# Second mixer: inputs with tokens on partitions, matrix-engine transposes in place of rearranging through memory, direct term in the kernel matrices

## The reference

```
u, z = split(rmsnorm(h) @ w_in, 2)              # 1024 columns each; u: 64 groups of 16 channels
x[t] = a * x[t-1] + B u[t]                      # complex, 64 states for each group
y = Re(C x) + d_skip * u                        # the last part is the direct term
y = gelu(y);  ga, gb = split(y @ w_glu, 2)
h = h + (ga * sigmoid(gb) * silu(z)) @ w_out
```

## Time and profile before

| what | value |
|---|---|
| median of three runs | 2049.64 us (2049.35 to 2049.81) |
| the profiled execution's own time | 2053.18 us |
| its span, first to last instruction | 2051.4 us |
| mean granted PE clock | 0.955 |
| PE busy | 1826.9 us (89%) |
| DVE, ACT, POOL busy | 1005.5, 816.8, 303.3 us |
| from the end of attention to the last output tile | 461.4 to 523.4 us |
| from there to the first glu product | 523.4 to 684.7 us |

### The profile page before, as it was taken

The page is one execution under the profiler, slowest core; times in us unless marked ns, Lnnn a source line. Parts: engine busy times, 40 slices in busy tenths (PEclk is TensorE's granted clock), DMA queues, the critical chain, the costliest instruction groups (busy, mean ns, idle before and its releaser), DMA issues.

```text
span 2051.4 us, 23580 instructions
## 1 busy us (share of the span) xinstructions
PE 1826.9 (89%) x9454; PEld 1450.1 (71%) x9454; DVE 1005.5 (49%) x1694; ACT 816.8 (40%) x1348; POOL 303.3 (15%) x376
## 2 busy tenths in 40 slices
PE   3488699997996999999799999999999969999996
PEld 2366578775775787786487777887777748888885
DVE  7647845665564446434434454445544364334323
ACT  4034356763313424333425545256632443223222
POOL 1347432546000000000000000012200021111000
PEclk9789799998998999999999999999999979999998
DMA  3154231005667422321032221321122212233231
GB/s 108 47 168 144 99 98 42 12 1 157 156 157 167 132 84 92 105 95 48 21 116 78 82 83 62 100 69 61 63 82 92 83 41 93 92 103 100 85 95 59
DMA packets 79230, 183.37 MB, mean 89 GB/s; under 512 B 24449, under 2 KB 35585, under 8 KB 77329
## 3 DMA queue, kind: packets, MB, share of 16 engines
q1 hardware_dynamic: 79120, 181.87, 28.7%
HBM read 165.58 MB, written 16.25 MB: 89 GB/s over the span
## 4 chain that ended last, share of the span: by engine, by line
PE 66%; DVE 17%; ACT 8%; DMA 4%; issue 2%; POOL 2%; SPq 1%; DVEq 0%; ACTq 0%; POOLq 0%
PE bank L822 16%; PE bank L823 16%; PE bank L824 15%; DVE wlo L1720 2%; PE bank L861 2%; PE bank L862 2%; PE bank L863 2%; PE bank L1003 2%; PE bank L981 2%; ACT whi L1249 1%; POOL Ps L2473 1%; ACT Ps L1619 1%; DVE Pb L1842 1%; DVE CA L1688 1%; PE bank L842 1%
## 5 line engine op out<-in xcount | busy, mean ns | idle before, releaser
L1720 DVE TENSOR_TENSOR wlo<-wraw,whi 128x1024 fp32r<-128x1024 f32 (+1 forms) x262 | 327.5, 1253 | 344.1 <-ACT whi L1249 342.7
L822 PE MATMUL bank<-Hh,whi 128*128 128x512 f32 (+2 forms) x1136 | 461.2, 406 | 24.0 <-DVE wlo L1720 13.2
L823 PE MATMUL bank<-Hl,whi 128*128 128x512 f32 (+2 forms) x1136 | 448.6, 395 | 0.0
L824 PE MATMUL bank<-Hh,wlo 128*128 128x512 f32 (+2 forms) x1136 | 448.2, 395 | 0.0
L1249 ACT ACTIVATE whi<-wraw 128x1024 fp32r<-128x1024 f32 (+1 forms) x262 | 271.1, 1040 | 373.0 <-PE bank L824 260.1
L822 PEld LDWEIGHTS bank<-Hh,whi 128*128 128x128 f32 (+2 forms) x1136 | 215.5, 190 | 84.5 <-DVE qs L1786 11.8
L824 PEld LDWEIGHTS bank<-Hh,wlo 128*128 128x128 f32 (+2 forms) x1136 | 215.3, 189 | 48.9 <-issue 0.6
L823 PEld LDWEIGHTS bank<-Hl,whi 128*128 128x128 f32 (+2 forms) x1136 | 215.8, 190 | 47.5 <-issue 2.7
L2466 POOL TENSOR_SCALAR bs<-dist 128x256 f32<-128x256 f32 x16 | 7.3, 457 | 831.8 <-DMA dist<-in_c_dist 831.1
L822 PE MATMUL bank<-Bh,whi 128*128 128x512 f32 x256 | 103.1, 403 | 2.2 <-DVE Bl L2244 2.2
L824 PE MATMUL bank<-Bh,wlo 128*128 128x512 f32 x256 | 102.1, 399 | 0.0
(11 more groups left out here) (368 smaller groups left out, 3044.7 us busy)
## 6 DMA issues: line engine op xcount, KB each, us to landing
wraw<-in_w_o SPq DMA_DIRECT2D x24, 512.0 KB, 3.5
wraw<-in_w_bgate SPq DMA_DIRECT2D x24, 512.0 KB, 3.4
wraw<-in_w_branch SPq DMA_DIRECT2D x24, 512.0 KB, 3.5
wraw<-in_w_fg SPq DMA_DIRECT2D x22, 512.0 KB, 3.4
wraw<-in_w_fu SPq DMA_DIRECT2D x22, 512.0 KB, 3.4
wraw<-in_w_s SPq DMA_DIRECT2D x16, 512.0 KB, 4.1
wraw<-in_w_glu SPq DMA_DIRECT2D x16, 512.0 KB, 3.6
wraw<-in_w_fd SPq DMA_DIRECT2D x16, 512.0 KB, 3.5
```

The source lines that it names most:

```text
L822: pe.matmul(o, wh[:, cols], hi(k), start=k == 0, stop=False)
L823: pe.matmul(o, wh[:, cols], lo(k), start=False, stop=False)
L824: m = pe.matmul(o, wl[:, cols], hi(k), start=False, stop=k == K - 1)
L1720: dve.tensor_tensor(c.wlo[q][:, 0:n], c.raw[i % RR][:, 0:n], c.whi[q][:, 0:n].bitcast(F32), S_).then_inc(*up(DID, ("wlo", i)))
```

## The change

The columns of `u` are computed the other way round: `tok_twin` takes 128 tokens as the stationary operand and 256 weight columns as the moving one, so that tokens lie on partitions. Four such steps `u0` to `u3` of 96 matmuls each take the place of eight `u` tiles. ACT evicts each bank with four copies (`ev_su`) into `Z`, with the factor 1/rms, which `rsS` has turned onto partitions; 16 transposes of 64x128 (`rows`) and two copies (ACT, DVE) give `U`. No memory is passed. The outputs are copied to `Yo` in a layout with 64 partitions, in four copies, and 16 transposes of 64x128 give y with channels on partitions; gelu reads it from PSUM. The direct term is added to the kernel matrix before it is stored (`prep_k` on DVE), so `finish` is gone. The shifted copies of `scratch_K` are made in memory during attention (`expand`), and `mT` comes in one DMA. `mW` has two buffers. `x_again` fetches one part of `X` per output tile, in that tile's step, and the first fetches come between these steps. Some working tiles move to other addresses.

```diff
+    def tok_twin(self, w, m, src):
+
+        keys = [(w, m, i) for i in range(2)]
+        for key in keys:
+            self.bank.take(key)
+        for j in range(2):
+            i = self.piece(w, (m, j), 0, 1024)
+            self.step("tok_twin", keys, i, j, src)
...
+            self.step("x_again", t)
             self.evict(("w_o0", t))
             self.step("split_h1", t)
             self.square("h1", t, 0, t == 0)
+            for kind, n, b in (("fetch_w", 2, 0), ("fetch_m", 3, 0), ("fetch_w", 5, 1)):
+                if t == n:
+                    self.step(kind, b)
...
+            if i in (16, 24, 32, 40):
+                self.step("expand", i // 8 - 2)
         self.drain()
-        self.step("x_again")
...
-        self.pair([("w_s5", 0), ("w_s5", 1)], "h1")
-        self.inv("h1", 0, 7, 0, 1.0 / D, "rs")
-
-        def u_tile(k):
-            if k > 1:
-                self.gemm("w_s5", k, "h1")
-            self.evict(("w_s5", k))
+
+        def inputs(b):
+            keys = self.tok_twin("w_su", b, "h1")
+            if b == 0:
+                self.inv("h1", 0, 7, 0, 1.0 / D, "rs")
+                self.early = keys
+                return
+            if b == 1:
+                self.bank.take("rsS")
+                self.step("rsS")
+                self.bank.give("rsS")
+                for key in self.early:
+                    self.evict(key)
+            for key in keys:
+                self.evict(key)
 
         def rows(b):
+            for i in range(2):
+                self.bank.take(("ut", b, i))
             self.step("rows", b)
+            for i in range(2):
+                self.bank.give(("ut", b, i))
...
-        order = ("u0 u1 r0 u2 u3 r1 s0 u4 w1 u5 r2 o0 s1 u6 w2 m2 u7 r3 t0 o1 s2 z0 w3 z1 m3 f0 t1 o2 s3 y0 z2 z3 f1 y1 "
-                 "t2 o3 z4 f2 y2 t3 z5 z6 z7 f3 y3")
+        fns = dict(u=inputs, r=rows, s=states, o=outputs, t=turned, z=z_tile, y=split_y, w=fetch_w, m=fetch_m)
+        order = ("u0 m1 u1 r0 s0 u2 r1 s1 w2 o0 u3 r2 s2 w3 m2 t0 o1 z0 r3 s3 m3 t1 o2 y0 z1 y1 z2 t2 y2 o3 z3 t3 y3 "
+                 "z4 z5 z6 z7")
...
+    def tok_twin(keys, i, j, src):
+        hi, lo = c.moving[src]
+        wh, wl = c.whi[plan.ring[i]], c.wlo[plan.ring[i]]
+        on.wait_ge(*at("wlo", i))
+        for t in range(4):
+            o = bank(keys[t // 2])[:, (t % 2) * 256:(t % 2) * 256 + 256]
+            if j == 0:
+                on.wait_ge(*before(plan.bank, keys[t // 2]))
+            rows = slice(t * 128, t * 128 + 128)
+            for kk in range(4):
+                k = j * 4 + kk
+                on.wait_ge(*at("lo", src, k))
...
+            done = [("used", i)] if t == 3 else []
+            if j == 1 and t % 2:
+                done.append(("tile", keys[t // 2]))
+            if done:
+                m.then_inc(*up(PE, *done))
...
+    def rsS():
+        b = bank("rsS")
+        on.wait_ge(*before(plan.bank, "rsS"))
+        on.wait_ge(*at("inv", "h1"))
+        for t in range(4):
+            for a in range(2):
+                x = pe.matmul(b[a * 64:a * 64 + 64, t:t + 1], c.rs[:, :].rearrange("p (n s) -> p s n", s=8)[:, 2 * t + a, :],
+                              c.ident[:, 0:1], start=True, stop=True)
+        x.then_inc(*up(PE, ("rsS",)))
+
+    def rows(b):
+        for i in range(2):
+            u = bank(("ut", b, i))
+            on.wait_ge(*before(plan.bank, ("ut", b, i)))
+            on.wait_ge(*at("Z", b, 1))
+            for g in range(8):
+                x = pe.transpose(u[:, g * 64:g * 64 + 64], c.Z[:, 8 * i + g, :, :].rearrange("p s n -> p (s n)"),
+                                 c.ident[0:64, 0:64])
+            x.then_inc(*up(PE, ("ut", b, i)))
...
-            for q in range(4):
-                x = pe.transpose(y[:, q * 128:q * 128 + 128], c.Yo[:, i, q * 128:q * 128 + 128], c.ident[:, :])
+            for k in range(8):
+                x = pe.transpose(y[:, k * 64:k * 64 + 64], c.Yo[:, i, k, :, :, :].rearrange("p q h n -> p (q h n)"),
+                                 c.ident[0:64, 0:64])
...
-        copy(c.Kp[:, :, 8:16, :].rearrange("p q k n -> p q (k n)"), k.rearrange("p (q n) -> p q n", q=4)).then_inc(
-            *up(DID, ("Kp", b), ("freed", ("kk", b))))
+        copy(c.Kp[:, :, 9:16, :].rearrange("p q k n -> p q (k n)"), k.rearrange("p (q n) -> p q n", q=4)[:, :, 16:128]).then_inc(
+            *up(DID, ("Kp", b)))
...
+    def ev_su(key):
+        _, b, i = key
+        on.wait_ge(*at("tile", key))
+        on.wait_ge(*at("rsSc"))
+        if b:
+            on.wait_ge(*at("ut", b - 1, 1))
+        for t in (2 * i, 2 * i + 1):
+            for a in range(2):
+                half = slice(a * 64, a * 64 + 64)
+                x = copy(c.Z[:, :, 2 * t + a, :],
+                         bank(key)[half, (t % 2) * 256:(t % 2) * 256 + 256].rearrange("p (g n) -> p g n", n=16),
+                         scale=c.rsS[half, t:t + 1])
+        x.then_inc(*up(DID, ("Z", b, i), ("freed", key)))
+
+    def rows(b):
+        on.wait_ge(*at("ut", b, 0))
+        copy(c.U[b][:, 0:8, :].rearrange("p g n -> p (g n)"), bank(("ut", b, 0))).then_inc(
+            *up(DID, ("U", b, 0), ("freed", ("ut", b, 0))))
...
-            copy(c.Yo[:, i, :], bank(("y", b, i))).then_inc(*up(DID, ("Yo", b, i), ("freed", ("y", b, i))))
+            for h in range(2):
+                half = slice(h * 64, h * 64 + 64)
+                x = copy(c.Yo[:, i, :, :, h, :].rearrange("p k q n -> p q k n"),
+                         bank(("y", b, i))[half, :].rearrange("p (q k n) -> p q k n", q=4, k=8))
+            x.then_inc(*up(DID, ("Yo", b, i), ("freed", ("y", b, i))))
 
     def turned(b):
         for i in range(2):
             on.wait_ge(*at("yt", b, i))
-            if b:
-                on.wait_ge(*at("dy", b - 1))
-            copy(c.Yt[:, 8 * i:8 * i + 8, :].rearrange("p g n -> p (g n)"), bank(("yt", b, i))).then_inc(
-                *up(DID, ("Yt", b, i), ("freed", ("yt", b, i))))
-
+            act.activation(c.Y[:, 2 * b + i, :], bank(("yt", b, i)), ACT.Gelu_apprx_tanh).then_inc(
+                *up(DID, ("gelu", 2 * b + i), ("freed", ("yt", b, i))))
...
+        dve.tensor_tensor(c.Kp[:, :, 8, :], k[:, :, 0:16], c.skip[:, b, :, :], A_).then_inc(
+            *up(DID, ("Kd", b), ("freed", ("kk", b))))
+
+    def rsS():
+        on.wait_ge(*at("rsS"))
+        dve.tensor_copy(c.rsS, bank("rsS")[:, 0:4]).then_inc(*up(DID, ("rsSc",), ("freed", "rsS")))
+
+    def rows(b):
+        on.wait_ge(*at("ut", b, 1))
+        dve.tensor_copy(c.U[b][:, 8:16, :].rearrange("p g n -> p (g n)"), bank(("ut", b, 1))).then_inc(
+            *up(DID, ("U", b, 1), ("freed", ("ut", b, 1))))
...
-    def finish(b):
-        for kk in range(2):
-            k = 2 * b + kk
-            dve.scalar_tensor_tensor(u, u, c.g_d[:, k:k + 1], y, M, A_).then_inc(
-                *up(DID, ("yd", k), ("freed", ("yi", b, kk))))
...
-    def x_again():
+    def x_again(k):
         for u in range(60, 64):
             on.wait_ge(*at("p", u, 1))
-        for k in range(KT):
-            sp.dma_start(c.X[:, k, :], I["xT"][k]).then_inc(*land(f"in_x{k}", ("x_again", k)))
+        sp.dma_start(c.X[:, k, :], I["xT"][k]).then_inc(*land(f"in_x{k}", ("x_again", k)))
...
+    def expand(b):
+        on.wait_ge(*at("K", b))
+        for st in range(8):
+            sp.dma_start(c.dT[b][st * 16:st * 16 + 16, :, :], c.dK[b][:, :, (8 - st) * 16:(16 - st) * 16]).then_inc(
+                *land(f"st_T{b}", *([("T", b)] if st == 7 else [])))
+
     def fetch_w(b):
-        if b:
-            on.wait_ge(*at("v", b - 1))
+        if b >= 2:
+            on.wait_ge(*at("v", b - 2))
+        else:
+            on.wait_ge(*at("pv", 63, 1))
         for n in range(4 * b, 4 * b + 4):
             on.wait_ge(*at("W", n))
-        sp.dma_start(c.mW[:, :, :, :].rearrange("p i q n -> p (i q n)"), c.dW[b]).then_inc(*land(f"turn{b}", ("W_in", b)))
+        sp.dma_start(c.mW[b % 2][:, :, :, :].rearrange("p i q n -> p (i q n)"), c.dW[b]).then_inc(
+            *land(f"turn{b}", ("W_in", b)))
 
     def fetch_m(b):
         CA, T = c.mCA[b % 2], c.mT[b % 2]
         if b >= 2:
             on.wait_ge(*at("y", b - 2, 1))
+        elif b == 1:
+            on.wait_ge(*at("tile", ("w_o0", 7)))
+        else:
+            on.wait_ge(*at("pv", 63, 1))
         on.wait_ge(*at("CAd", b))
         sp.dma_start(CA[:, :, :, :, :].rearrange("p i q k n -> p (i q k n)"), c.dCA[b]).then_inc(*land(f"mats{b}"))
-        on.wait_ge(*at("K", b))
-        for st in range(8):
-            sp.dma_start(T[st * 16:st * 16 + 16, :, :], c.dK[b][:, :, (8 - st) * 16:(16 - st) * 16]).then_inc(
-                *land(f"mats{b}", *([("mats", b)] if st == 7 else [])))
-
-    def split_g0(t):
-        if t == 7:
-            on.wait_ge(*at("pv", 63, 1))
-            fetch_w(0)
-            fetch_m(0)
-
-    def s5_in():
-        free_after("fence", 0)
-        fetch_m(1)
-
-    def rows(b):
-        for kk in range(2):
```

(39 more changed lines are left out.)

89 lines of the change are left out of this document (43 added, 46 removed).

## The result

The changed kernel takes 2063.86 us (median of 4 runs, 2062.78 to 2066.22) against 2049.49 us of the kernel before on the same chip: a ratio of 1.0072, 95% interval 1.0055 to 1.009. Timed once more later it gave 1.0076, 1.0062 to 1.009. That is slower by 0.7%; the forecast was 2060 us, inside its range of 2042 to 2072.

A forecast was written before the change was run, and what follows sets the result against it. PE, busy 89% of the span, was taken as the bound. Output tiles +15.0 us and S5 -5.1 us gave 9.9 us more, span 2051.4 to 2061.3; on the median, 2049.6 + 9.9, about 2060 us, range 2042 to 2072.

The forecast's parts named there:

- Part A: Output tiles of the first mixer: late reload of `X` moves the last `Hl` from 526.8 to 541.8, costing 15.0 us.
- the wait: Output tiles 2 to 7: DVE waits 4.1 us each for `X(t)`, 24.6 us in all; bounds 3.15 and 5.
- Part B: From the last `Hl` to the first glu product: 152.8 us against 157.9 before, a gain of 5.1 us.
- 8.7 us after `u1`: S5: PE idle 8.7 us while `rsS`, ACT's copies of `u0` and `u1` and the copy to `U` run.
- 4.55 twice: S5, `s1` and `s2`: PE waits 4.55 us each, the copy to `U` standing behind ACT's eight copies.
- 1.4: S5, `s3`: PE waits 1.4 us behind the eviction and silu of `z0`.
- A transpose: S5: 128 transposes of 64 rows at 0.08 us each, 10.2 us; bounds 0.065 and 0.13 each.
- Rival 1: Output tiles: reload of `X` lands before DVE asks, the 24.6 us vanish, 2035 us; chance 15%.
- the excess under POOL's table: First output tiles: 6.5 of 7.4 us of DVE's longer instructions kept while POOL computes its table; bounds 3 and 7.4.
- Rival 2: S5: ACT copies with scattered addresses take 0.90 us, 32 exposed copies cost 14 us more, 2074 us; chance 11%.
- rival 3: Waits at lower bounds, 3.15 us and 0.38 us a copy: 2051 us, no change; chance 10%.
- Rival 4: Attention: DVE's wait in `prep_k` delays a `wlo`, up to 6 us more, 2066 us; chance 6%.

The follow-up runs named there:

- the control: The changed kernel once more, unedited: ratio 1.0076 to the kernel before, median 2065.6 us.
- run 6: The changed kernel with each of the 128 new transposes of 64 rows issued twice: 2073.1 us.
- run 4: The changed kernel with ACT's copy into `U(b)` ahead of its eight copies of `u(b+1)` into `Z`: 2049.4 us.
- run 1: The changed kernel with all eight parts of `X` asked for at the attention's end: 2040.8 us.
- run 2: The changed kernel with `X(t+2)` instead of `X(t)` asked for in the step of tile t: 2041.1 us.
- run 3: The kernel before with only the late reload, `X(t)` asked for in the step of tile t: 2076.0 us, ratio 1.0135.
- run 8: run 7 plus POOL's last table step held until the last `Hl`, listed ahead of the fence that opens S5: 2031.7 us.
- run 7: The changed kernel with the edits of run 1 and run 4 together: 2025.1 us.
- run 9: run 7 plus DVE copying the second half of `u(0)` into `Z`, and `z0` behind the transposes of step 3: 2019.9 us.
- run 10: run 7 plus POOL's last table step held until the last `Hl`, listed behind the fence that opens S5: 2023.1 us.
- run 11: run 9 plus POOL's last table step held until the last `Hl`, listed behind the fence that opens S5: 2017.3 us.

## Why the prediction was right

**Part A was predicted at +15.0 us and is +17 to +19.** The mechanism is the predicted one, row for row: the load, issued 0.03 us after the `wlo` ahead of the add, and `X(t)` right behind it; six waits; adds 9.2 us apart in the last tiles (531.01 to 540.17); PE with slack. From tile 2's first product to the last `Hl` I had 541.8 - 472.8 = 69.0 us; it is 73.2 in the profiled execution and 71.3 in the control. The term that was mis-sized is the wait: 24.6 us predicted, 28.9 measured. The five usual waits were a little longer than my 4.1 (4.2 to 4.7, 1.2 us in sum), and the sixth was 7.22, 3.1 us more; that one is 5.20 in the control. Everything else in the sum, 44.4 us, measures 44.3. The span hides this: the profiled execution reached tile 2 at 470.0 instead of 472.8, and the control, at 475.5, shows that this start moves by itself.

**Part B was predicted at 152.8 us and is 152.7 and 152.6.** Its terms hold: idle time 19.2 and 0.5 predicted, 20.0 measured; the rest 133.1 predicted, 132.7 measured. Of the waits, 8.7 us after `u1` are 4.16 + 4.83; 4.55 twice are 4.68 and 4.83; 1.4 is 1.54. A transpose was taken at 0.08 us and costs 0.062 to 0.076 at a granted clock of 1.00 (runs of 16 in 1.21 us, and run 6). The copies into `Z` take 0.470 us each, where the nearest row had 0.474. Run 4 shows that the order on ACT causes the waits and that two of the three slow runs of products go with them.

**The sum, and where it was lucky.** +19.2 (A) - 5.1 (B) - 2.7 (start) - 1.7 (after the first glu product) = 9.7 us, and the spans differ by 9.6, where I had 9.9. That these agree so well is luck. Part A came out 4.2 us dearer than predicted, and 4.4 us came back from the start and the rest, which I had taken as unchanged and don't count to the change: the start differs by 5.5 us between two traces of the changed kernel, and with the old S5 the rest is 1366.7 us in one trace and 1363.0 in the other. The medians don't share this: they are 14.4 us apart, and the ratios 1.0072 and 1.0076 are 14.8 and 15.6 us, against the predicted 10. So the forecast of 2060 was about 4 us low. The step that was short is the wait in part A, 4.1 us in the sum against 4.8 in the mean of the six (4.5 in the control).

**The rivals.** Rival 1, the hidden reload, did not happen; made to happen in runs 1 and 2, it gives 2041 us and not the 2035 that I worked out. The step that failed there: I took the excess under POOL's table for a constant 6.5 us. It is 4.4 us more when DVE has no waits (tile 2's first product to the last `Hl` is 48.8 us in run 1 against 44.4), because more of DVE's work then lies beside the table. Rival 2, slow scattered copies, is refuted by 0.469 to 0.472 us for all 32; rival 3 by the waits, all above their lower bound of 3.15 us. Rival 4, `prep_k`'s wait on DVE, would show as a late start of the output tiles. The two traces of kernels with the old `prep_k` (before and run 3) start tile 0 at 461.4 us both. Of the twelve with the new one, eleven start it at 458.7 to 461.1 and the control at 464.2. So nothing in these traces speaks for a cost of `prep_k` or of `expand`, though no experiment removed either.

## What to carry to other kernels

A transfer that an in-order queue issues behind a load waits for all that the load waits for; look which compute instruction that is, and if it is the one just before the transfer's use, the whole landing time is in the chain, in each turn of the loop. Two turns of distance made it free. An instruction that replaces a round trip through memory is itself cheap; what is queued ahead of it on its engine decides, and here one change of order was worth 14 us. When a step is moved out of another's way, move it past the fences too, and ask whether the engine that sets the end will still be the one that was freed.

## What the runs showed of the hardware

- POOL's products and sums on tiles outside the banks and DVE's operations with two such inputs held each other up: `wlo` 3.42 us and `nacc` 2.83 us beside the table, 1.23 and 0.69 with it out of the way (runs 1 and 8), while DVE's adds that read one input from a bank stayed at 0.67 to 0.69 us in both. POOL's last step of four products and two sums took 15.5 us beside such work (run 1) and 13.3 beside an idle DVE (run 8). The Trainium skill ("SBUF — State Buffer", "SBUF: two separate sides") has this as an exclusive lock on a shared pair of ports, taken by DVE for two inputs from SBUF; the rows agree, down to the DVE instruction that ends 0.55 to 1.08 us after POOL's (run 1).
- One more transpose with 64 rows and 128 columns loaded and 64 columns moving cost PE 0.062 us in a row of them at a granted clock of 1.00, less than I expected from any row of the kernel before, and 0.106 us at 0.50 (run 6).
- After gaps of 4.2 to 4.8 us PE's next 64 small products took 3.4 to 3.7 us, at a granted clock of 0.50 to 0.55; after gaps of 0.9 to 1.5 us mostly 2.08, at 1.00. The exception is `states(0)` in runs 4, 7, 9, 10 and 11: behind a gap of 0.9 us they took 3.4 to 3.7. In run 4 the clock had been 0.50 since the 16 transposes ahead of that gap, which took 1.97 us behind a gap of 4.16 (1.21 later).
- The same kernel reached the same add at 469.5 us in one execution and at 475.0 in another. The distance B was 152.7 and 152.6 us in the same two executions.
